# Two transformer blocks on one core: the mixing stage turns X unscaled, and its steps in another order

## The reference

```
x = x + 0.5 * swiglu(rms_norm(x, ffn1_norm), gate, up, down)       # 2816 wide
h = rms_norm(x, mix_norm)
a, g, q, k, v = split(h @ w_in)                                    # 512 columns each
conv_out = silu(rms_norm(causal_depthwise_conv31(a * sigmoid(g)) + conv_b, conv_norm))
q = rms_norm(q per head half of 64, q_norm);  k the same with k_norm
p_m = softmax(causal(q_m k_m^T / 8 + rel_bias)),  m = 0, 1         # 4 heads
diff_out = rms_norm((p_0 - lam * p_1) @ v, subln) * (1 - lam_init)
x = x + concat(conv_out, diff_out) @ w_out
x = x + 0.5 * swiglu(rms_norm(x, ffn2_norm), ...)
```

## Time and profile before

| | |
|---|---|
| time, median of 3 runs | 1810.5 us (1810.07 to 1811.17) |
| the profiled execution | 1811.22 us |
| its span, first to last instruction | 1809.4 us |
| PE, DVE, ACT, POOL busy | 97%, 67%, 50%, 16% of the span |
| granted TensorE clock, mean | 0.992 |
| first layer's mixing stage | about 990 to 1119 us |
| second layer's | about 1491 to 1620 us |

### The profile page before, as it was taken

How to read it: one execution, slowest core, us unless ns; L and a number is a source line. 1 busy time by engine, 2 the same in 40 slices (tenths; PEclk the granted TensorE clock), 3 DMA queues, 4 the chain that set the end, 5 groups by cost and what they waited for, 6 DMA issues and landing times.

```text
span 1809.4 us, 25402 instructions
## 1 busy us (share of the span) xinstructions
PE 1758.0 (97%) x9839; PEld 1502.4 (83%) x9839; DVE 1208.4 (67%) x1594; ACT 911.7 (50%) x1221; POOL 287.7 (16%) x155
## 2 busy tenths in 40 slices
PE   8999999999999999999999998999999999989999
PEld 7757888899897788878888977888888889778887
DVE  5756766778676775576665794666666667946665
ACT  4544444545455444445445656544554456565443
POOL 2000300376241040000000741000000006410000
PEclk9999999999999999999999999999999999999999
DMA  9223655554502576535554432655465554316552
GB/s 302 102 70 124 220 191 186 152 181 156 198 1 83 156 238 194 188 129 195 194 193 163 164 116 70 209 185 188 161 209 185 186 185 164 117 47 209 192 194 102
DMA packets 203965, 293.95 MB, mean 162 GB/s; under 512 B 6426, under 2 KB 169728, under 8 KB 203888
## 3 DMA queue, kind: packets, MB, share of 16 engines
q1 hardware_dynamic: 200768, 285.62, 47.6%
q0 software_dynamic: 2688, 6.47, 1.4%
q10 hardware_dynamic: 432, 0.79, 0.1%
HBM read 291.81 MB, written 1.05 MB: 162 GB/s over the span
## 4 chain that ended last, share of the span: by engine, by line
PE 87%; DVE 8%; ACT 3%; issue 1%; DMA 0%; POOL 0%; SPq 0%; ACTq 0%; DVEq 0%
PE acc L1864 27%; PE pg L1864 15%; PE pg L1927 12%; PE pg L1931 12%; PE pg L1930 6%; PE pg L1928 6%; PE acc L2338 1%; DVE acc L1743 1%; PE pg L2134 1%; ACT w_hi L793 1%; DVE w_lo L1252 1%; PE pg L2322 1%; PE pg L2324 1%; DVE stats L1307 1%; PE pg L1975 1%
## 5 line engine op out<-in xcount | busy, mean ns | idle before, releaser
L1252 DVE TENSOR_TENSOR w_lo<-w_raw,w_hi 128x2048 fp32r<-128x2048 f32 x231 | 539.1, 2334 | 182.2 <-ACT w_hi L793 170.6
L793 ACT CAST w_hi<-w_raw 128x2048 fp32r<-128x2048 f32 x270 | 515.6, 1910 | 68.5 <-PE pg L1864 25.2
L1864 PE MATMUL acc<-w_hi,op 128*128 128x512 f32 x1536 | 496.6, 394 | 8.2 <-DVE op L1829 6.4
L1927 PE MATMUL pg<-op,w_hi 128*128 128x512 f32 x960 | 383.2, 399 | 7.7 <-DVE op L1278 3.8
L1931 PE MATMUL pg<-op,w_hi 128*128 128x512 f32 x960 | 380.8, 397 | 0.0
L1864 PEld LDWEIGHTS acc<-w_hi,op 128*128 128x128 f32 x1536 | 290.4, 189 | 70.0 <-issue 12.6
L1864 PE MATMUL acc<-w_lo,op 128*128 128x512 f32 x768 | 300.7, 392 | 0.0
L695 POOL TENSOR_TENSOR w_lo<-w_raw,w_hi 128x2048 fp32r<-128x2048 f32 x39 | 179.8, 4613 | 743.5 <-DVE w_lo L1252 615.4
L1930 PE MATMUL pg<-op,w_lo 128*128 128x256 f32 x960 | 267.9, 279 | 0.0
L1928 PE MATMUL pg<-op,w_lo 128*128 128x256 f32 x960 | 267.0, 278 | 0.0
L1864 PE MATMUL pg<-op,w_hi 128*128 128x256 f32 x1232 | 229.2, 286 | 2.8 <-DVE op L1278 1.2
(11 more groups left out here) (314 smaller groups left out, 1845.2 us busy)
## 6 DMA issues: line engine op xcount, KB each, us to landing
w_raw<-in_mlp_w SPq DMA_DIRECT2D x64, 1024.0 KB, 5.5
w_raw<-in_ffn_w_gate SPq DMA_DIRECT2D x44, 1024.0 KB, 5.1
w_raw<-in_ffn_w_up SPq DMA_DIRECT2D x44, 1024.0 KB, 5.1
w_raw<-in_ffn_w_down SPq DMA_DIRECT2D x44, 1024.0 KB, 4.8
w_raw<-in_ssm_w_in SPq DMA_DIRECT2D x24, 1024.0 KB, 5.3
w_raw<-in_w_in SPq DMA_DIRECT2D x20, 1024.0 KB, 5.0
w_raw<-in_attn_w_in SPq DMA_DIRECT2D x9, 1024.0 KB, 9.2
w_raw<-in_ssm_w_out SPq DMA_DIRECT2D x8, 1024.0 KB, 4.8
```

Of the source, the lines that this page charges most:

```text
L793: act.copy(w_hi[:, u % RING, :], w_raw[:, u % RING, :]).then_inc(hi_ready, 1)
L1252: dve.tensor_tensor(w_lo[:, s, :], w_raw[:, s, :], w_hi[:, s, :].bitcast(F32), ALU.subtract) \
L1864: ins = pe.matmul(psum, l, r, start=first and i == 0, stop=last and i == 2)
L1927: pe.matmul(bank, hi, joined, start=k == 0, stop=False)
```

## The change

The mixing stage's X is turned by column halves like the other two, unscaled. The reciprocal rms per token is spread over partitions (`spread_tokens`) and multiplied into the gates before the sigmoid and again into the gates after it (which scales the values), into V at its copy, and for q and k only the epsilon is scaled (`tok_eps`). Head sums come out as tokens by heads (narrow matmuls), with the root and reciprocal on 8 columns; the query's factor goes into the score step's scalar, the key's is spread back by `key_spread`. The units' order is gate pair 1, value pair 1, q, k, q, k, gate pair 2, value pair 2, V; score steps, exponentials and head mixing lie among the last projections, and their order is written out on every engine. DVE's taps run channel groups 0 and 1 first, then 2. TensorE's 31 taps lie behind V. The diagonals have other homes and four groups. The output product takes the attention's units first, token half by token half, then the convolution's. The convolution's sum comes out by tokens and is spread by a product. The table of Sqrt is loaded at the head of `turn_columns`. In the first block's attention tail ACT's splits of output units 2 and 3 move to s = 14 and s = 16, behind `turned_head`, and DVE's to s = 15 and s = 17. The head mixing's instructions (`mix_head`) are those of before. The diff below is cut to its core; most removed lines are left out.

```diff
-MIX_COLS = [2 * U, 0, 3 * U, U] + [2 * CCH + i * U for i in (0, 2, 1, 3, 4, 5)]
...
+MIX_COLS = [2 * U, 0] + [2 * CCH + i * U for i in (0, 2, 1, 3)] + [3 * U, U] + [2 * CCH + i * U for i in (4, 5)]
+
+
+DIAGS = [0, 8, 16, 24, CK]
...
-                if s == AQ + 2:
-                    split(U_ATT_OUT + 2)
-                if s == AQ + 7:
-                    split(U_ATT_OUT + 3)
                 if AQ <= s - 3 < AQ + BH:
                     turned_head(s - 3)
                 if s >= 13 and s % 2 == 1:
                     pair_hi((s - 5) // 2)
+                if s == 14:
+                    split(U_ATT_OUT + 2)
+                if s == 16:
+                    split(U_ATT_OUT + 3)
...
-                rms_std(4 + 3 * l + 2, x_new, 4 * (4 + 3 * l))
-                turn(f"mix_{l}", COL["mix"] + 8 * l, None)
...
+                for n in range(7):
+                    if n == 1:
+                        act.wait_ge(mix_spread, l + 1)
+                        act.copy(token_rstd, acc[:, 3, 0:T]).then_inc(mix_rb, 1)
+                        gate_columns(0)
+                    if 3 <= n <= 6:
+                        head_evac(n - 1)
+                    split(U_MIX[l] + n + 2)
+                    if n < 3:
+                        diag_taps(n)
+                    else:
+                        head_root(n - 1)
+                    if n in (4, 6):
+                        head_expand(l, n // 2 - 2)
+                    if n == 5:
+                        diag_taps(3)
+                    if n == 6:
+                        act.wait_ge(cconv, 3 * l + 2)
+                        conv_square(0)
+                gate_columns(1)
+                exp_step(0)
+                exp_step(1)
+                exp_step(2)
+                split(U_MIX[l] + 9)
+                exp_step(3)
+                split(U_MIX_OUT[l])
+                exp_step(4)
+                exp_step(5)
+                turned_mix(0)
+                split(U_MIX_OUT[l] + 1)
+                exp_step(6)
+                act.wait_ge(first_tile, l + 2)
+                act.activation(V2[:, 0, :], acc[:, 0, :], ACT.Identity, scale=rstd[:, 0:1]).then_inc(v_ready, 1)
+                turned_mix(1)
+                exp_step(7)
+                link(act.activation(part[:, 0:1], lnb[:, 0:1], ACT.Sqrt))
+                act.wait_ge(unit_done, U_MIX[l] + 10)
+                act.activation(V2[:, 1, :], acc[:, 1, :], ACT.Identity, scale=rstd[:, 1:2]).then_inc(v_ready, 1)
+                turned_mix(2)
+                turned_mix(3)
+                o2_square(l, 0)
+                o2_square(l, 1)
+                o2_high(l, 0)
+                o2_high(l, 1)
...
+                dve.tensor_tensor(tok_eps[:, 0, :], std[:, :], std[:, :], ALU.mult).then_inc(mix_rstd, 1)
+                dve.wait_ge(mix_rstd, l + 1)
+                link(dve.tensor_scalar(tok_eps[:, 1, :], tok_eps[:, 0, :], EPS2, None, ALU.mult))
+                dve.tensor_scalar(tok_eps[:, 0, :], tok_eps[:, 0, :], EPS2 / SCALE ** 2, None, ALU.mult) \
+                    .then_inc(mix_eps, 1)
...
+                    link(dve.tensor_tensor(gate, gate, token_rstd.unsqueeze(1).broadcast_to([P, 2, T]), ALU.mult))
...
+                def score_step(s):
+                    i, h, b = 8 * l + s, s // 2, s % 4
+                    dve.wait_ge(sc2_done, i + 1)
+                    if s == 0:
+                        dve.wait_ge(qk_rstd, 4 * l + 1)
+                    if s == 4:
+                        dve.wait_ge(qk_rstd, 4 * l + 3)
+                    for a, z, qt in ((0, P, 0), (P, 384, 1)):
+                        r = ((h % 2) * TT + qt) * 2 + s % 2
+                        ins = dve.scalar_tensor_tensor(out=prob2[:, b, a:z], in0=pg[:, s % 2, a:z],
+                                                       scalar=qr[:, h // 2, r:r + 1], in1=rbias[:, h, a:z],
+                                                       op0=ALU.mult, op1=ALU.add)
+                    ins.then_inc(sc2_taken, 1)
+                    dve.wait_ge(sc2_taken, i + 1)
+                    dve.tensor_reduce(m2[:, s, 0:1], prob2[:, b, 0:P], AX.X, ALU.max)
+                    link(dve.tensor_reduce(m2[:, s, 1:2], prob2[:, b, P:384], AX.X, ALU.max))
+                    dve.tensor_scalar(n2[:, s, :], m2[:, s, :], -1.0, None, ALU.mult).then_inc(mx2_ready, 1)
...
+                gate_scale(0)
+                gated_columns(0)
+                convolve(22)
+                head_rstd(2)
+                convolve(16)
+                head_rstd(3)
+                convolve(15)
+                head_rstd(4)
+                convolve(3)
+                key_norm(0)
+                convolve(4)
+                score_step(0)
+                convolve(2)
+                head_rstd(5)
+                score_step(1)
+                score_step(2)
+                gate_scale(1)
+                key_norm(1)
+                score_step(3)
+                mix_head(0)
                 gated_columns(1)
...
+                score_step(4)
+                mix_head(1)
+                convolve(3)
+                score_step(5)
+                convolve(4)
+                score_step(6)
+                convolve(2)
+                mix_head(2)
+                score_step(7)
+                convolve(4)
+                mix_head(3)
+                convolve(7)
+                o2_scale(0)
+                convolve(4)
+                o2_scale(1)
+                o2_low(0)
+                o2_low(1)
+                convolve(7)
                 dve.wait_ge(cstd, l + 1)
...
+                    if 3 <= n < 7:
+                        qk_sums(4 * l + n - 3)
+                    if n == 5:
+                        key_spread(2 * l)
+                    if n == 6:
+                        score2(1)
+                    if n == 7:
+                        score2(3)
+                    feature_chunk(u, bank[:, T:2 * T], 1).then_inc(unit_done, 1)
+                    if n == 5:
+                        score2(0)
+                    if n == 6:
+                        score2(2)
+                        key_spread(2 * l + 1)
+                score2(4)
+                u = U_MIX[l] + 8
+                take(u)
+                pe.wait_ge(qk_std, 4 * l + 4)
+                wide_tile(u, 0, acc[:, 0, :], 0)
+                score2(5)
+                pe.wait_ge(qk_ready, 2 * l + 2)
+                wide_tile(u, 0, acc[:, 1, :], 1).then_inc(unit_done, 1)
+                mix_turn(0)
+                score2(6)
+                take(u + 1)
+                wide_tile(u + 1, 1, acc[:, 0, :], 0).then_inc(first_tile, 1)
+                mix_turn(1)
+                score2(7)
+                wide_tile(u + 1, 1, acc[:, 1, :], 1).then_inc(unit_done, 1)
+                conv_taps(0, 4)
+                o2(l, 0)
+                mix_turn(2)
+                o2(l, 1)
+                conv_taps(4, 8)
+                mix_turn(3)
+                o2(l, 2)
+                conv_taps(8, 12)
+                o2(l, 3)
+                conv_taps(12, 24)
+                o2_turn(0)
+                conv_taps(24, CK)
+                o2_turn(1)
+                u = U_MIX_OUT[l]
+                take(u)
+                pe.wait_ge(o2_ready, 2 * l + 1)
+                for i in (0, 1, 4, 5):
+                    output_part(u, 12, i, True, False)
+                pe.wait_ge(csq, 2 * l + 2)
+                for t in range(TT):
+                    for c in range(4):
```

More of the change, by code:

```diff
@@ L640, in _ @@
                     load(U_MIX[l] + n, columns(v_mix[l], c) if n < 8 else half_rows(v_mix[l], MIX_COLS[8], n - 8))
-                for n in range(OUT_UNITS):
-                    load(U_MIX_OUT[l] + n, rows(v_mix_out[l], n))
+                for n, g in enumerate((2, 3, 0, 1)):
+                    load(U_MIX_OUT[l] + n, rows(v_mix_out[l], g))
                 swiglu(U_FFN[2 * l + 1], ffn[2 * l + 1])
@@ L1711, in _ @@
                 swiglu(U_FFN[2 * l], HG_FFN[2 * l])
-                residual(U_MIX[l] - 1, 5 + 3 * l, True, norm=True)
-                turn(f"mix_{l}", COL["mix"] + 8 * l, U_MIX[l] + 1)
-                def gated_columns(n):
+                residual(U_MIX[l] - 1, 5 + 3 * l, True, columns=(f"mix_{l}", COL["mix"] + 8 * l))
+                split(U_MIX[l] + 1)
+                for t in range(TT):
+                    rstd_make(6 + 3 * l, t)
+                dve.tensor_tensor(tok_eps[:, 0, :], std[:, :], std[:, :], ALU.mult).then_inc(mix_rstd, 1)
@@ L1897, in project, with wide_tile @@
                 ins.then_inc(unit_done, 1)
+            def wide_tile(u, half, bank, t):
+                ts = slice(t * P, t * P + P)
+                for k in range(4):
+                    j = 4 * half + k
+                    ins = three(bank, wslice(u, k * 2 * U, (k + 1) * 2 * U),
+                                (op_hi[:, j, ts], op_lo[:, j, ts]), j == 0, j == KC - 1, swap=True)
+                return ins
             def project_wide(u, half, banks, first_sem=None, second_free=None, count=0):
```

(19 more changed lines are left out.)

566 lines of the change are left out of this document (268 added, 298 removed).

## The result

The changed kernel takes 1833.1 us (median of 4, 1830.8 to 1833.4) against 1810.8 us: ratio 1.0121, 95% interval 1.0103 to 1.0138. The forecast was 1827 us in a range of 1800 to 1838. The profiled execution has a span of 1829.0 us.

A forecast was written before the change was run, and what follows sets the result against it. In the mixing stage, the order in which DVE and ACT answer TensorE was taken to count, not their totals. 1811.2 + 21.0 (two layers) - 4.2 (attention tail) = 1828.0, as a median 1827 us; range 1800 to 1838.

The forecast's parts named there:

- the likeliest case: Whole kernel: exposed DVE instructions in the mixing stages are held by POOL's splits; 1820 to 1833 us, chance 0.54.
- turn by halves: Start of the mixing stage: turning X by column halves lets the first unit end earlier; 2.4 us won a layer.
- TensorE's own work: Mixing stage: added spreads and head sums, less a cheaper convolution sum; net 1.5 us more a layer.
- spread: Token spread: DVE's square of std is held by the third unit's split, so TensorE waits 1.95 us.
- head 1's turn: Before head 1's turn: step 4's negation and head 1's coefficient are held by splits; TensorE waits 5.9 us.
- first value product: Before the first value product: step 6's negation held, then exponentials, table load, second V tile; TensorE waits 8.0 us.
- convolution's sum: Before the convolution's sum: the last 7 taps queue behind the attention output's second low half; TensorE waits 3.1 us.
- slow products: Mixing stage: slow TensorE products after a stand; 0.9 us a layer added, from the same walk on the old order.
- The walk down each engine's order: Mixing stage: durations carried down each engine's written order to place waits; with ffn2's turn, +10.5 us a layer.
- the rival at 1835 to 1838: Mixing stages: small reciprocals held too, or slow matmuls follow the long stands twice more a layer; chance 0.12.
- The rival that holds don't matter: Mixing stages: splits fall between exposed instructions or small ones slip by; -3.7 us a layer, 1799 us, chance 0.22.
- The open bound, reciprocals held too: Mixing stage: small DVE reciprocals beside a split might be held as well; 4.8 us more a layer, no row showing one.

The follow-up runs named there:

- the kernel with the two splits moved: Changed kernel with the first two output units' low halves made by DVE at idle places instead of POOL: 1814.6 us, ratio to before 1.0018.
- the last kernel: Changed kernel with last taps earlier, three small places undone, three output units' low halves by DVE, and no score-step negations: 1792.2 us, ratio to before 0.9901.
- the kernel with the cut splits: Changed kernel with POOL's twelve splits of each mixing stage cut from 2048 to 8 columns: 1800.8 us, ratio to before 0.9947.
- both probes: Kernel before with 13, then 14, small DVE instructions of several forms set among the first mixing stage's taps: 1828.9 us, then 1810.3 against 1811.0.
- three repairs: Changed kernel with last taps earlier, three small places undone, and the first two output units' low halves made by DVE: 1797.5 us, ratio to before 0.9926.
- and the last output unit's low half: The kernel of the three repairs, with the last output unit's low half made by DVE too: 1796.8 us, ratio to before 0.9924.

## Why the prediction was right

Size and sign came out: 22.3 us lost, 16.8 forecast (1833.1 us, at the upper edge of the likeliest case's 1820 to 1833); the mechanism and each of its three places are there. That the size came out is in part luck: the forecast had the waits 6.3 us a layer too long and the slow products behind them 6.6 too short. Step by step, per layer:

| step | predicted | measured in the first layer |
|---|---|---|
| turn by halves | -2.4 | first unit ends 10.9 us after the half-turn, 13.15 before: -2.3 |
| TensorE's own work | +1.5 | 128.7 us from there, less 13.7 waits and 7.5 slow = 107.5; before, 114.8 less 7.4 and 2.7 = 104.7: +2.8 |
| spread | wait 1.95 | 1.60 |
| small waits | 1.1 | 0.3 |
| head 1's turn | wait 5.9 | 4.08 |
| first value product | wait 8.0 | 4.63 |
| convolution's sum | wait 3.1 | 3.06 |
| slow products | 0.9 | 7.5 |
| ffn2's turn | +0.9 | +0.9 |
| attention tail, once | -4.2 | -4.35 |

The slow products are distances of starts less those of the same matmuls at full clock: behind head 1's wait 7.00 us (1062.14 to 1069.14) for 4.14 (1053.77 to 1057.91), behind the value product's 3.14 (1075.67 to 1078.81) for 1.74 (the kernel with the two splits moved, 1070.54 to 1072.28), behind the sum's 7.87 (1099.00 to 1106.87) for 4.64 (the last kernel, 1084.06 to 1088.70), so 2.9, 1.4 and 3.2. The prediction's 3.0 for the kernel before is 2.7 by the same measure. With the old waits and slow products the sum is -2.3 + 2.8 + 13.7 + 7.5 - 7.4 - 2.7 = 11.6, the stage's loss of 11.7 to the rounding.

The walk down each engine's order held: set beside the trace with the first unit's end as zero, it had step 4's negation at 1055.4 (trace 1055.0), the end of the second hold at 1063.1 (1062.3), step 5 at 1065.9 (its maxima at 1065.6, its negation at 1066.3), the third split at 1070.7 catching step 6's negation (1069.7, the same one). Two sizes were off and nearly cancelled. The term "0.9 is added below (slow products after a stand)" was an eighth of what came: the prediction had the rows for it, and gave it to the rival at 1835 to 1838 instead of to the forecast; that part of the rival came true. And because TensorE came slow out of the first wait, it was late at the second (in that frame 1076.8 instead of 1074.7). That is 2.1 us of the 3.4 by which this wait was shorter; the rest is that ACT was done with the second V tile at 1081.4 instead of 1082.7. Both belong together: a wait must be priced with the slow stretch that can follow it, and the next wait less that stretch. Can, because the stretch didn't always come: in the kernel with the two splits moved, the matmul behind the 3.11-us wait is at full clock in the first layer (0.46 us) and slow in the second (0.77 us behind another wait of 3.11). The spread was seen right, but undoing it won only 1.1 of its 1.6 us: 0.5 came back as a longer wait for the next low half (0.29 to 0.79).

TensorE's own work is 1.3 us more than counted. It is about the same in the kernel with the cut splits (125.2 less 10.9, waits of 3.9 and 3.2 slow is 107.2) and in the last of the repaired ones, which has nothing slow in its first layer (120.1 less 10.9 and waits of 2.0 is 107.2). Where it lies was not found.

The rival that holds don't matter is refuted by the cut and by the two moved splits; had it been so, the kernel would have come near the 1799 it gave (1800.8 without the splits). The open bound, reciprocals held too, is refuted by both probes.

The Trainium skill (SBUF — State Buffer, section Who interferes with whom) names two classes that share the port pair with GpSimd, VectorE's 2-port modes and instructions with two SBUF inputs. The probes agree on both: scalar product and copy, 3.81 and 3.61 us; two SBUF inputs, 4.09 and 4.00 us; with PSUM 0.16.

## What to carry to other kernels

Before moving small vector work to another place in the order, list what GpSimd runs there. Beside the one form of GpSimd instruction that these kernels have there (a subtraction of two SBUF tensors, 4.6 us), scalar products and copies from SBUF to SBUF and instructions with two SBUF inputs stop until it ends, even with two elements, and everything queued behind them stops with them; an input in PSUM, a reduction or a reciprocal passes. Deleting the instruction that was caught gave 2.0 and 2.7 us of the stages' 11.7 and 12.0, since the next is caught; moving two long ones to an idle place of another engine gave 9.9 and 9.2. And price a wait of TensorE with the slow products that can follow it: 1.4 to 3.2 us behind waits of 3 to 5 us in the changed kernel's first layer, and nothing behind the one of 3.11 us in the first layer of the kernel with the two splits moved.

## What was not expected of the hardware

A copy of two elements is held too (3.61 us). And the clock behind a short wait did not repeat. Four kernels wait 0.86 to 0.88 us before the convolution's sum, and in the 8 us from about there the granted clock was, in the first and second layer:

| kernel | wait 20 us earlier | clock |
|---|---|---|
| last taps earlier | 4.41, 5.01 | 0.79, 1.00 |
| three repairs | 1.41, 1.44 | 0.79, 1.00 |
| and the last output unit's low half | 1.40, 1.43 | 0.60, 0.79 |
| and no negations | 0.35, 0.37 | 1.00, 0.79 |

Between the first layers of the last two kernels it is worth 2.7 us of the stage from the sum to the next spread (1084.16 to 1091.54, and 1084.06 to 1088.70). One profile each: a difference of that size between two kernels can be this alone.
